# A hybrid decoder layer on one core: experts' further rows in tiles of 64 whose high and low parts share one stationary operand

## The reference, cut to what matters

```
expert_ids = grp[:, None] * EXPERTS_PER_GROUP + top_i            # (1024, 2)
combine = jnp.sum(jax.nn.one_hot(expert_ids, N_EXPERTS) * weights[..., None], axis=1)
for e in range(N_EXPERTS):                                        # 16
    h = jax.nn.silu(t @ w_gate[e]) * (t @ w_up[e])                # 1024 -> 512
    y = y + combine[:, e:e + 1] * (h @ w_down[e])                 # 512 -> 1024
```

## Time and profile before

| | |
|---|---|
| runs, median (lowest, highest) | 1030.34 us (1028.25, 1030.80) |
| span of the profiled execution | 1032.5 us |
| mean granted TensorE clock | 0.947 of full speed |
| busy: PE, DVE, ACT, POOL | 88%, 60%, 51%, 24% |
| first product of the expert stage | at 564.5 us |
| first product of the last tile | at 998.2 us |
| scatter-adds of finished tiles | 24 |

### The profile page before, as it was taken

How to read it: one execution, slowest core, us unless ns; L and a number is a source line. 1 busy time by engine, 2 the same in 40 slices (tenths; PEclk the granted TensorE clock), 3 DMA queues, 4 the chain that set the end, 5 groups by cost and what they waited for, 6 DMA issues and landing times.

```text
span 1032.5 us, 16968 instructions
## 1 busy us (share of the span) xinstructions
PE 910.3 (88%) x5042; PEld 756.7 (73%) x5043; DVE 617.7 (60%) x1245; ACT 528.9 (51%) x953; POOL 248.2 (24%) x368
## 2 busy tenths in 40 slices
PE   3889999999999957999822999999999999999993
PEld 2768888888898845788711787787787877787773
DVE  2657656666666572333657735744758499663991
ACT  2464754646637470222132645654657488573871
POOL 3101011011010100000054224314315246323352
PEclk9999999999999958899955999999999999999998
DMA  8620010100100313344642967867869699966963
GB/s 258 221 65 21 22 41 0 41 20 20 41 0 22 141 64 103 133 152 143 213 174 81 407 179 255 257 162 245 278 157 390 174 356 393 352 178 196 330 230 61
DMA packets 58122, 169.68 MB, mean 164 GB/s; under 512 B 12744, under 2 KB 15088, under 8 KB 58096
## 3 DMA queue, kind: packets, MB, share of 16 engines
q1 hardware_dynamic: 50384, 143.13, 38.5%
q0 software_dynamic: 7712, 26.24, 10.9%
HBM read 142.96 MB, written 26.38 MB: 164 GB/s over the span
## 4 chain that ended last, share of the span: by engine, by line
PE 63%; DVE 13%; issue 11%; ACT 5%; DVEq 3%; DMA 2%; POOL 2%; SPq 0%; ACTq 0%; POOLq 0%
PE bank_j L913 12%; PE bank_j L915 12%; PE bank_j L914 11%; DVE w_low L1673 8%; PE bank_j L1009 6%; PE bank_j L1020 3%; PE bank_o L1000 3%; PE bank_t L907 2%; PE bank_t L993 2%; DVE q_sb L1647 1%; ACT w_high L653 1%; PE bank_x L1192 1%; DVE lg L1667 1%; ACT rows_high L653 1%; PE bank_s L985 1%
## 5 line engine op out<-in xcount | busy, mean ns | idle before, releaser
L913 PE MATMUL bank_j<-w_high,rows_high 128*128 128x512 f32 x640 | 257.5, 402 | 11.2 <-DVE w_low L1368 8.9
L915 PE MATMUL bank_j<-w_high,rows_low 128*128 128x512 f32 x640 | 251.8, 393 | 0.0
L914 PE MATMUL bank_j<-w_low,rows_high 128*128 128x512 f32 x640 | 251.6, 393 | 0.0
L913 PEld LDWEIGHTS bank_j<-w_high,rows_high 128*128 128x128 f32 x640 | 121.8, 190 | 40.5 <-issue 12.8
L545 POOL TENSOR_TENSOR tick<-mhalf 1x1 f32<-1x1 f32 x146 | 84.0, 578 | 278.5 <-ACT lg L850 136.7
L915 PEld LDWEIGHTS bank_j<-w_high,rows_low 128*128 128x128 f32 x640 | 121.5, 190 | 26.4
L914 PEld LDWEIGHTS bank_j<-w_low,rows_high 128*128 128x128 f32 x640 | 122.0, 191 | 24.0
L1673 DVE TENSOR_TENSOR w_low<-w_res,w_high 128x1024 fp32r<-128x1024 f32 x96 | 112.7, 1216 | 13.8 <-ACT w_high L653 13.8
L653 ACT ACTIVATE w_high<-w_res 128x1024 fp32r<-128x1024 f32 x96 | 96.1, 1059 | 8.3 <-PE bank_j L915 8.0
L907 PE MATMUL bank_t<-ident,hn 128*128 128x128 f32 x328 | 45.2, 283 | 38.6 <-DMA hn<-ffn_in,row_g 24.4
L907 PEld LDWEIGHTS bank_t<-ident,hn 128*128 128x128 f32 x328 | 40.0, 147 | 43.7 <-issue 39.6
(11 more groups left out here) (307 smaller groups left out, 1751.4 us busy)
## 6 DMA issues: line engine op xcount, KB each, us to landing
w_res<-in_w_gate_dram SPq DMA_DIRECT2D x48, 512.0 KB, 5.0
w_res<-in_w_up_dram SPq DMA_DIRECT2D x48, 512.0 KB, 5.3
bias<-in_w_down_dram SPq DMA_DIRECT2D x32, 512.0 KB
slot_b<-in_w_gate_dram SPq DMA_DIRECT2D x16, 512.0 KB
PT<-in_w_up_dram SPq DMA_DIRECT2D x16, 512.0 KB
gmix<-in_w_down_dram SPq DMA_DIRECT2D x16, 512.0 KB
h<-in_w_down_dram SPq DMA_DIRECT2D x16, 512.0 KB
hn<-in_x_dram SPq DMA_DIRECT2D x8, 512.0 KB, 3.3
```

The costliest lines, as they stand in the source:

```text
L913: pe.matmul(out_, ah, bh, start=start, stop=False)
L914: pe.matmul(out_, ah, bl, start=False, stop=False)
L915: return pe.matmul(out_, al, bh, start=False, stop=stop)
```

## The change

An expert's last tile keeps 128 rows and three products per step; all its tiles ahead of that have 64 rows and two products per step. For such a tile the 64 rows are gathered twice, into partitions 0 to 63 and 64 to 127. The transposed rows are kept as [high 128 | low 128] per k, and columns 64 to 191 of it are one stationary operand: the high part of the upper copy and the low part of the lower copy. It is multiplied with the high and then the low weights, so that the upper 64 rows of the bank hold high x (high + low) and the lower 64 hold low x (high + low). The two halves are added: ACT copies the upper half down (`fold_hi`), DVE adds the lower (`fold_lo`), and only then come SiLU (`silu_half`) and the product with up (`hidden_half`). The result of down is folded in the same way (`weigh_half`).

Three more things change. In PE's program the places of the hidden transposes move: `hidden_T(t, 0)` comes after k = 5 (128-row tiles) or k = 6 (64-row tiles) of half 1, and `hidden_T(t, 1)` ahead of c = 1 or c = 2 of down. The table has 64 rows of 258 columns in place of 128 of 130, is read back by two transfers, and a DVE copy arranges the upper half. And the first `row_g` is written by DVE, ahead of its first split, not by POOL.

For the default inputs nine 64-row tiles (two for expert 4) take the place of eight 128-row ones: 25 tiles in all.

```diff
-            pool.tensor_copy(row_g[:, :], rows[:, 0, 0:1]).then_inc(pool_rowg, 1)
-            pool.wait_ge(pool_rowg, 1)
+            pool.wait_ge(dve_rows, 2)
             gather()
...
+            def fold_hi(t, half):
+                act.wait_ge(pe_gup, (FC + 1) * t + (1 if half == 0 else FC + 1))
+                wait(act, dve_mh, 2 * t)
+                cp(fold[:, half * FF:(half + 1) * FF], (J0, J1)[half][HP:, :]).then_inc(act_fold, 1)
+            def silu_half(t, half):
+                act.wait_ge(dve_fold, 2 * t + half + 1)
+                act.activation(sg[0:HP, half * HF:(half + 1) * HF], fold[:, half * FF:half * FF + HF],
+                               ACT.Silu).then_inc(act_silu, 1)
...
+            def weigh_half(t):
+                act.wait_ge(pe_dnp, FC * (t + 1))
+                act.wait_ge(dve_wt, t + 1)
+                wait(act, dve_y, t)
+                act.activation(y_fold[0], S1[HP:, :], ACT.Copy, scale=wt_t[HP:, 0:1])
+                act.activation(y_fold[1], O0[HP:, :], ACT.Copy, scale=wt_t[HP:, 0:1]).then_inc(act_y, 1)
...
+            def half_tile(t):
+                act.activation(warm[:, 0:1], warm[:, 1:2], ACT.Silu)
+                for half in range(2):
+                    fold_hi(t, half)
+                    silu_half(t, half)
+                    hidden_hi(t, half, HP)
+                rows_hi(t + 1)
+                weigh_half(t)
...
+            def both(out_, a, bh, bl, start, stop):
+                pe.matmul(out_, a, bh, start=start, stop=False)
+                return pe.matmul(out_, a, bl, start=False, stop=stop)
...
-                        if half == 1 and k == KC // 2 - 1:
+                        if half == 1 and k == split_at:
                             hidden_T(t, 0)
...
                 rows_T(t + 1)
-                hidden_T(t, 1)
                 wait(pe, act_y, t)
                 wait(pe, dve_y, t)
                 for c in range(FC):
+                    if c == down_at:
+                        hidden_T(t, 1)
                     if c % 2 == 0:
                         pe.wait_ge(dve_hT, 2 * t + c // 2 + 1)
...
-                with pe.Fori(first, last + 1) as t:
-                    tile(t, e)
+                with pe.If(first < last):
+                    with pe.Fori(first, last) as t:
+                        tile(t, e, HP, KC - 2, 2)
+                tile(last, e, P, 5, 1)
...
+            def half_tile(t):
+                wait(dve, act_y, t)
+                wait(dve, dve_y, t)
+                col = dve.value_load(tabi[0:1, bass.ds(t + ROWS, 1)], min_val=0, max_val=TCOLS - 2)
+                dve.tensor_copy(wt_t[:, 0:1], rows[:, bass.ds(col, 1), 1:2].rearrange("p a c -> p (a c)")
+                                .bitcast(F32)).then_inc(dve_wt, 1)
+                for half in range(2):
+                    fold_lo(t, half)
+                    hidden_half(t, half)
+                    hidden_lo(t, half, HP)
+                rows_lo(t + 1)
+                weigh_half(t)
...
+            dve.wait_ge(ld_rows, 32)
+            upper = rows[HP:, 0:NE * HT, :].rearrange("p (e a) c -> p e a c", a=HT)
+            dve.tensor_copy(upper[:, :, 0, :], upper[:, :, 1, :]).then_inc(dve_rows, 1)
+            dve.wait_ge(dve_tab, 1)
+            dve.wait_ge(dve_rows, 1)
+            col = dve.value_load(tabi[0:1, ROWS:ROWS + 1], min_val=0, max_val=TCOLS - 2)
+            dve.tensor_copy(row_g[:, :], rows[:, bass.ds(col, 1), 0:1].rearrange("p a c -> p (a c)")).then_inc(dve_rows, 1)
             for i in range(2 * FC):
                 split_lo(0, i)
             rows_lo(0)
             for i in range(2 * FC, PIECES):
                 split_lo(0, i)
-            dve.wait_ge(ld_rows, 16)
```

More of the change, by code:

```diff
@@ L91, in hymba_layer_program @@
         whi, wlo = sb("w_high", [P, PIECES * PW], F32R), sb("w_low", [P, PIECES * PW], F32R)
-        mxh, mxl = sb("rows_high", [P, KC, P], F32R), sb("rows_low", [P, KC, P], F32R)
+        rows_split = sb("rows_split", [P, KC, 2, P], F32R)
+        mxh, mxl = (rows_split[:, :, i, :] for i in range(2))
+        rows_pair = rows_split[:, :, :, :].rearrange("p k s n -> p k (s n)")[:, :, HP:HP + P]
         MX = [(mxh, mxl), tuple(w[:, OUTP * PW:(OUTP + 1) * PW].rearrange("p (k n) -> p k n", k=KC)
@@ L114, in hymba_layer_program @@
         overlaid.close()
-        mhh, mhl = sb("hidden_high", [P, FC, P], F32R), sb("hidden_low", [P, FC, P], F32R)
+        hid_split = sb("hidden_split", [P, FC, 2, P], F32R)
+        mhh, mhl = (hid_split[:, :, i, :] for i in range(2))
+        hid_pair = hid_split[:, :, :, :].rearrange("p k s n -> p k (s n)")[:, :, HP:HP + P]
         slot_b = sb("slot_b", [P, G * P + KVW + 64 + 2 * P + 2 * KVW])
@@ L636, in inner_tiles @@
                     with pool.Fori(first, last) as t:
-                        tile(t)
+                        tile(t, HP)
                 return last
             with pool.Fori(0, NE - 1) as e:
-                tile(inner_tiles(e))
+                tile(inner_tiles(e), P)
             end = inner_tiles(NE - 1)
-            tile(end)
+            tile(end, P)
             pwait(st_y, 16 * end + 16)
@@ L888, in inner_tiles @@
                     with act.Fori(first, last) as t:
-                        tile(t, lambda a, b: None)
+                        half_tile(t)
                 return last
@@ L1611, in _ @@
             cnt = off_e[one, T_, :]
[L1612 to L1615 removed]
+            NH = HT - 2
+            cmp = new(NE * NH)[one, :].rearrange("p (e k) -> p e k", e=NE)
+            thr = new(NH)[one, :]
+            chain(dve.tensor_scalar(thr, iota_f[one, 0:NH], float(HP), float(P), ALU.mult, ALU.add))
+            tt(cmp, cnt.unsqueeze(2).to_broadcast([1, NE, NH]), thr.unsqueeze(1).to_broadcast([1, NE, NH]),
                ALU.is_gt)
@@ L1667, in weigh, with weigh_half @@
                 dve.tensor_scalar(yb[:, HALF:], O0[:, :], wt_t[:, 0:1], None, ALU.mult).then_inc(dve_y, 1)
+            def weigh_half(t):
+                dve.wait_ge(act_y, t + 1)
+                dve.wait_ge(dve_wt, t + 1)
+                dve.wait_ge(st_y, 16 * t)
+                for half, b in enumerate((S1, O0)):
+                    ins = dve.scalar_tensor_tensor(yb[0:HP, half * HALF:(half + 1) * HALF], b[0:HP, :], wt_t[0:HP, 0:1],
+                                                   y_fold[half], ALU.mult, ALU.add)
+                ins.then_inc(dve_y, 1)
             def split_lo(e, i):
```

142 lines of the change are left out of this document (81 added, 61 removed).

## The result

The kernel after took 1038.18 us (median of 4 runs, 1036.88 to 1040.52) beside 1029.71 for the kernel before (4 runs, 1028.25 to 1030.80): a ratio of 1.0081, 95% interval 1.0057 to 1.0106, so 5.9 to 10.9 us slower. The forecast was 1034.4. The profiled execution took 1037.78 us.

What follows compares the result with a forecast made beforehand. It took DVE's chain of splits to bind at 15 expert boundaries. Stage +7.4, start -3.5 and setup +0.2 made +4.1 us, so the median 1030.34 would become 1034.4, range 1025 to 1044.

Steps and rivals of the forecast that it cites:

- What binds: Expert stage: at 15 expert boundaries DVE's chain of splits up to the next hidden product binds, not PE.
- Across a boundary to 128 rows, 19.21 unchanged: Step between first hidden transposes across an expert boundary into a 128-row tile, seven times: stays 19.21 us.
- What moves is the place in the tile: Same 128-row boundary step: splits and first hidden transposes come 1.36 us later in the tile, step length unchanged.
- No wait is in it: Kernel before, PE's tile from 603.69: its 18.03 us are all products and transposes, without a wait.
- Into a 64-row tile, 20.28: Step across an expert boundary into a 64-row tile, eight times: 20.28 us for 19.21, together +8.6.
- Out of it, 16.25, and 13.53 into expert 4's second: Steps from 64-row tiles, PE binding, 1.26 us wait ahead of c = 2: 16.25 for 18.09 (eight, -14.7); additional step 13.53.
- The clock: Rival: PE's clock halves after 2.7 us idle in 64-row tiles behind boundaries, eight times 1.8 us, 1049; chance 0.15.
- The stage: Expert stage, sum of all steps: +7.4 us.
- The start, -3.5: Stage start, from reading the table to the first product: first product at 561.0 for 564.54, gain 3.5 us.
- that rival: Stage start: POOL's first gather waits for the end of DVE's splits, first product 6.9 us later, 1041; chance 0.12.
- The setup, +0.2: Setup ahead of the first norm: POOL's fill and iota of the wider table take 0.2 us more for both.
- PE binds after all: Rival, expert stage: splits not in the way, so PE sets the steps; 1013 us; chance 0.05.

Runs made afterwards that it cites:

- e5: Kernel before with the first hidden transposes after k = 5 of half 1 instead of k = 3; 1016.56 us, ratio 0.9843.
- e9: Kernel before with every split of an expert's piece covering only 512 of its 1024 columns, so the result is wrong; 1008.97 us, ratio 0.9764.
- e6: Kernel before with the hidden transposes in the changed kernel's places for 128-row tiles (after k = 5, ahead of c = 1); 1023.62 us, ratio 0.9944.
- e7: Kernel after with ten idle products ahead of the first hidden transposes of each 64-row tile; 1037.41 us, ratio 1.0076.
- e1: Kernel before once more, unchanged, for a second profile; 1031.24 us, ratio 0.9995.
- e10: Kernel after with every split of an expert's piece covering only 512 of its 1024 columns, so the result is wrong; 993.8 us, ratio 0.9620.
- e3: Kernel after with the 128-row tiles' hidden transposes back in their old places (after k = 3, straight behind the next rows' transposes); 1034.44 us, ratio 1.0020.
- e4: Kernel after, 128-row tiles with first hidden transposes after k = 5, second straight behind the next rows' transposes; 1029.03 us, ratio 0.9971.
- e2: Kernel before with the first row numbers written by DVE ahead of its first split, not by POOL; 1024.14 us, ratio 0.9950.
- e12: e4 with down splits spread over an expert's first 64-row tile, and 64-row tiles' second hidden transposes ahead of c = 1; 1012.80 us, ratio 0.9788.
- e11: e5 and e2 together: kernel before, first hidden transposes after k = 5, first row numbers by DVE; 1008.62 us, ratio 0.9763.

## Why the prediction came out as it did

The result lies inside the range and on the side that was forecast, 3.8 us above the forecast.

- *What binds.* Right: DVE's chain from the second hidden pair over ten splits. e5 and e9 each remove the 15 waits without changing a product.
- *Across a boundary to 128 rows, 19.21 unchanged.* They took 0.27 less than before on average, -1.9 us over seven. The step that failed is "What moves is the place in the tile", and with it "No wait is in it" of the tile before: a wait of 0.19 ahead of the second transposes, counted in the earlier trace rows as part of `rows_T`'s 1.09, goes when c = 0 stands before it. e6 measured it by itself.
- *Into a 64-row tile, 20.28.* 20.11: DVE came free after 18.48 rather than 18.75, for the same reason, and the tail of fold, SiLU and product took 1.62 for 1.53. The term +8.6 was +7.2.
- *Out of it, 16.25, and 13.53 into expert 4's second.* 16.06 with the clock up, and 13.3. The wait ahead of c = 2 came in all nine tiles: 1.15 from transposes to product, for 1.26. The term -14.7 was -16.1 without the clock.
- *The clock.* The forecast's sum had none of it, the rival had eight falls of 1.8. There were three of 1.5 to 1.6, +4.7 us. The trigger that I named, a single idle time between 1.3 and 3.8, was too simple, as e7 shows. The Trainium skill ("TensorE: Matmul & The Clock Gate", on HAM oscillation) warns of short bursts between waits. The trace agrees, with e7's four products between waits of 0.89 and 1.06, though in four tiles of eight only.
- *The stage.* 7.2 - 16.1 + 13.3 - 1.9 + 4.7 = +7.2, for +7.4 forecast. That the sum came out right is luck: the tiles' credits against the forecast (1.4, 1.4, 0.2 and 1.9) and the clock's debit of 4.7, which was not in it, nearly cancel. First and last tile add 0.6.
- *The start, -3.5.* -2.7 against the profile before, -1.5 against e1's. The gather took 1.14 in the burst and wasn't held to its end, so that rival fell. The term mis-sized is the read of the table: DVE's arranging copy starts 3.29 us behind the first issue (548.03), for 2.4, and so the first split 4.67 behind it, for 3.7.
- *The setup, +0.2.* +0.7: the fill took 0.31 for 0.20, the iota 0.77 where the earlier trace rows have 0.24 for half the columns on twice the partitions, and the first norm came 0.68 later (12.89 for 12.21).
- *PE binds after all.* It didn't; e10 shows that it nearly would with half the splits.

The three terms that the profiles give add up to +5.8 (+6.3 against e1) for the forecast's +4.1. The measured +8.5 has another 2.2 to 2.7 that lie in no part of the change that the traces show, about what executions of one kernel differ by (1028.25 to 1030.80 before); this stays open. So of the 3.8 us by which the forecast was missed, the traces account for about two.

## What to carry to other kernels

Before removing work from an engine, follow the cycle between two equal points of the loop and look at which engine has no gap in it: work taken from another engine comes back as waits, and new steps (here fold, SiLU, product) are priced by what they queue behind, not by their own duration. Try the places of the hand-overs in the unchanged kernel first: one loop index was worth 1.6% here, twice what the change cost, and most of what 64-row tiles gain after it is paid back by the additional tile (15.8 and 13.4). Edits that ride along should be run alone: the change's places gained 6.5 us in the kernel before (e6) and cost 6 in its own (e3), and its start gained 1.5 to 2.7 in a change that lost.

## What was unexpected of the hardware

- The clock fell to 0.50 behind two short waits with four products between (e7), while a single 1.32 had left it at 1.00, and so had a single 2.54 (e10, one tile). Of eight tiles alike in every wait it fell in three (after) or four (e3, e4, e7).
- POOL's first copy of `row_g` took 7.01 us before, 5.87 in e1 (the same program), 2.83 after and 3.02 in e2. Each ended 0.03 to 0.05 us behind the last split of DVE's burst (555.78 and 555.74 before, 558.62 and 558.57 after), whenever it had begun. The same holds for e3, e5 to e9 and e12; with the splits halved (e9) the burst was over sooner and the copy took 1.49, and where the burst was over before the copy began (e10) it took 0.18. In e4 and e11 the copy was through after 0.76 and 0.68, at the end of the split that ran, as the 1.18 of the earlier trace rows were; what lets it through there stays open. The first gather, a transfer that POOL issues, took only 1.13 to 1.20 inside such bursts (after, e2 and the other runs in which DVE writes the first row numbers). So the rival's wait for the end of the burst exists, but for the copy and not for the gather. The Trainium skill ("GPSIMD Engine Reference", 2.1 Instruction dispatch) has the first call of a freshly loaded kernel pay a load of some 6 us that no record shows. The copies of 7.01 and 5.87 would fit that; those of 2.83, 3.02 and 1.49 do not, and the burst's end fits all five.
